# A fused diffusion trunk layer in fp32: rotation tables with the gains multiplied in, differential norms by pairs, row transposes in the middle of a unit, branch weights split in the fourth unit, router logits one unit later

## The reference, cut to what matters

```python
def trunk_layer(l, x, cond, ctx, rope_a, rope_b, p):       # once for 128 prompt rows, once for 512 latent rows
    sh1, sc1, g1, sh2, sc2, g2 = split(silu(cond) @ w_ada + b_ada, 6)
    h = ln_plain(x) * (1 + sc1) + sh1
    aq, ak, av, bq, bk, bv, ga, gb = split(h @ w_in)        # 1024 x 6656
    bq = rms_norm(bq, b_q_g); bk = rms_norm(bk, b_k_g)      # per head of 64
    if rope: aq, ak, bq, bk = apply_rope(each)              # pairs: x1*c - x2*s, x1*s + x2*c
    o_a = diff_attention(aq, kA, vA, lam)                   # 8 heads, two maps: softmax1 - lam * softmax2
    #     then rms_norm(o, subln_g) * (1 - lambda_init), per head of 128
    o_b = gqa_attention(bq, kB, vB)                         # 16 query heads, 4 key heads
    merged = sigmoid(ga) * (o_a @ w_br_a) + sigmoid(gb) * (o_b @ w_br_b)
    x = ln_affine(ALPHA * x + g1 * (merged @ w_o), ln1_g, ln1_b)
    h = ln_plain(x) * (1 + sc2) + sh2
    y = hier_moe(h)     # router logits h @ [w_coarse | w_fine]; best group, its two best experts of four, of 16 in all
    return ln_affine(ALPHA * x + g2 * y, ln2_g, ln2_b), (ak, av, bk, bv)
```

## Time and profile before

| | |
|---|---|
| median of 3 runs | 1377.57 us (1375.84 to 1379.34) |
| the profiled execution's own time | 1376.48 us |
| its span, first to last instruction | 1374.6 us |
| mean granted TensorE clock | 0.952 |
| TensorE matmul busy | 1241.4 us (90%) |
| TensorE weight loads busy | 998.6 us (73%) |
| VectorE busy | 964.2 us (70%) |
| ScalarE busy | 657.8 us (48%) |
| GpSimd busy | 205.9 us (15%) |
| chain that ended last | TensorE 80%, VectorE 10%, DMA 4% |

### The profile page before, as it was taken

One profiled execution on the slowest core, in us unless ns is written; L12 is line 12 of the kernel. 1 busy time (PEld: TensorE's weight loads), 2 busy tenths in 40 slices (PEclk: granted clock), 3 DMA queues, 4 the chain that ended last, 5 costly groups with the idle time before them and its releaser, 6 DMA issues.

```text
span 1374.6 us, 20497 instructions
## 1 busy us (share of the span) xinstructions
PE 1241.4 (90%) x6673; PEld 998.6 (73%) x6673; DVE 964.2 (70%) x1746; ACT 657.8 (48%) x1049; POOL 205.9 (15%) x312
## 2 busy tenths in 40 slices
PE   7999999999999899998997999993699999999940
PEld 4777777777888788887876787773588888888830
DVE  5765521838571688888878535778889999999938
ACT  1522222223322577776763222113478888888812
POOL 0023221020232000011111001000111111122101
PEclk9999999999999999999999999995799999999975
DMA  9877664462646678642005433436899999999925
GB/s 348 283 245 238 207 222 169 153 214 85 201 137 187 180 195 223 187 128 85 27 25 182 131 120 138 169 144 252 299 332 370 372 381 391 388 382 381 336 108 146
DMA packets 150338, 301.05 MB, mean 219 GB/s; under 512 B 20380, under 2 KB 31196, under 8 KB 150264
## 3 DMA queue, kind: packets, MB, share of 16 engines
q1 hardware_dynamic: 122424, 232.72, 49.5%
q0 software_dynamic: 21920, 62.13, 14.5%
q10 hardware_dynamic: 5920, 5.24, 1.3%
HBM read 258.71 MB, written 53.38 MB: 227 GB/s over the span
## 4 chain that ended last, share of the span: by engine, by line
PE 80%; DVE 10%; DMA 4%; issue 2%; ACT 2%; SPq 1%; POOL 0%; DVEq 0%; POOLq 0%; ACTq 0%
PE psum_pair L1705 8%; PE psum_pair L1707 8%; PE psum_pair L1706 8%; PE psum_pair L1807 6%; PE psum_pair L1968 5%; PE psum_pair L1970 5%; PE psum_pair L1969 5%; PE psum_pair L1872 4%; PE psum_pair L1873 3%; PE psum_pair L1874 3%; PE psum_pair L1818 3%; PE psum_pair L1833 3%; PE psum_pair L1983 3%; PE psum_pair L1985 3%; PE psum_pair L1984 3%
## 5 line engine op out<-in xcount | busy, mean ns | idle before, releaser
L1705 PE MATMUL psum_pair<-w_parts,h_hi 128*128 128x512 f32 x520 | 207.8, 400 | 3.0 <-DVE h_lo L1253 3.0
L1707 PE MATMUL psum_pair<-w_parts,h_lo 128*128 128x512 f32 x520 | 204.2, 393 | 0.0
L1706 PE MATMUL psum_pair<-w_parts,h_hi 128*128 128x512 f32 x520 | 203.9, 392 | 0.0
L1110 DVE TENSOR_TENSOR w_parts<-w_raw,w_parts 128x1024 fp32r<-128x1024 f32 x72 | 83.3, 1220 | 91.2 <-ACT w_parts L835 91.1
L975 ACT ACTIVATE p_unnormed<-psum_pair,minus_max 128x640 f32<-128x640 f32 (+1 forms) x160 | 113.4, 712 | 67.2 <-DVE minus_max L1325 65.9
L1807 PE MATMUL psum_pair<-k_bundle,q_bundle 128*128 128x512 f32 (+1 forms) x576 | 123.2, 342 | 13.9 <-ACT p_unnormed L975 9.4
L1325 DVE TENSOR_REDUCE minus_max<-psum_pair 128x1 f32<-128x640 f32 (+1 forms) x160 | 111.8, 715 | 31.4 <-PE psum_pair L1807 28.9
L1705 PEld LDWEIGHTS psum_pair<-w_parts,h_hi 128*128 128x128 f32 x520 | 98.5, 189 | 30.9 <-issue 11.6
L1707 PEld LDWEIGHTS psum_pair<-w_parts,h_lo 128*128 128x128 f32 x520 | 98.4, 189 | 21.1
L1807 PEld LDWEIGHTS psum_pair<-k_bundle,q_bundle 128*128 128x128 f32 x576 | 88.6, 194 | 33.8 <-issue 20.6
L1706 PEld LDWEIGHTS psum_pair<-w_parts,h_hi 128*128 128x128 f32 x520 | 98.6, 190 | 19.7
(11 more groups left out here) (338 smaller groups left out, 2569.5 us busy)
## 6 DMA issues: line engine op xcount, KB each, us to landing
w_raw<-in_w_gate_up SPq DMA_DIRECT2D x76, 512.0 KB, 9.1
w_raw_c<-in_w_gate_up SPq DMA_DIRECT2D x72, 512.0 KB, 10.1
w_raw_b<-in_w_down SPq DMA_DIRECT2D x72, 512.0 KB, 9.2
w_raw<-in_w_in SPq DMA_DIRECT2D x52, 512.0 KB, 8.9
ada_raw<-in_w_ada SPq DMA_DIRECT2D x32, 512.0 KB, 7.4
k_bundle<-k_transposed SPq DMA_DIRECT2D x28, 384.0 KB, 8.5
q_transposed<-turned_staging POOLq DMA_DIRECT2D x40, 256.0 KB, 6.2
ada_raw_early<-in_w_ada SPq DMA_DIRECT2D x16, 512.0 KB, 8.8
```

What stands on the lines that cost most here:

```text
L1110: dve.tensor_tensor(w_parts[b % 2][:, 1, c], w_raw[:, c], w_parts[b % 2][:, 0, c].bitcast(F32), ALU.subtract).then_inc(lo_done, 1)
L1705: pe.matmul(out, a_hi, hi, start=kk == 0, stop=False)
L1706: pe.matmul(out, a_hi, lo, start=False, stop=False)
L1707: return pe.matmul(out, a_lo, hi, start=False, stop=kk == KD - 1)
```

## The change

Seven edits. (1) `gain_tables` multiplies the rotation tables by the gains once, and bq and bk of latent rows are rotated by those tables, without the product with the gain. (2) `norm_o` becomes `norm_sum` (one tile) and `norm_rows` (one or two tiles at once); tiles 1 and 2 and tiles 3 and 4 are normed as pairs, and the order on VectorE and ScalarE at the start of the branches is written out. (3) `turn_o(v + 1)` stands in the middle of unit v (after 6 of 8 steps for v = 0, after 4 otherwise). (4) The branch weights' next block is split at v % 5 == 3 instead of 0. (5) The first unit of each block waits for the weights chunk by chunk. (6) The logits of tile tt - 2 stand between the two halves of tile tt; the last two come at the end. (7) `take_logits` follows suit.

```diff
+        cos_g = sb("rope_cos_gain", [P, 2, TL, HD], F32, s12)
+        sin_g = sb("rope_sin_gain", [P, 2, TL, HD // 2], F32, s12)
+        nsin_g = sb("rope_minus_sin_gain", [P, 2, TL, HD // 2], F32, s12)
...
-        for tt in range(NT + 1):
-            if tt < NT:
-                tail_no["wo", tt, 0], tail_no["wo", tt, 1] = n, n + 1
-                n += 2
+        for tt in range(NT):
+            tail_no["wo", tt, 0] = n
+            n += 1
+            if tt >= 2:
+                tail_no["L", tt - 2] = n
+                n += 1
+            tail_no["wo", tt, 1] = n
+            n += 1
...
@@ ScalarE
-                        act.wait_ge(on_done, z)
+                        act.wait_ge(osum_done, z)
...
-                    square(v + 2)
-                if v % NT == 0:
+                if v == 0:
+                    square(2)
+                if v == 1:
+                    square(3)
+                    square(4)
+                if v % NT == 3:
                     split_hi(branch_block(v) + 1)
...
@@ VectorE
+            def gain_tables():
+                for i, g in enumerate((g_q, g_k)):
+                    halves = g[:].rearrange("p (e two) -> p e two", two=2)
+                    dve.tensor_tensor(cos_g[:, i], cosd[:], over(g[:], 1, [P, TL, HD]), ALU.mult)
+                    dve.tensor_tensor(sin_g[:, i], sind[:], over(halves[:, :, 0], 1, [P, TL, HD // 2]), ALU.mult)
+                    link(dve.tensor_tensor(nsin_g[:, i], nsin[:], over(halves[:, :, 1], 1, [P, TL, HD // 2]), ALU.mult))
...
-                        link(dve.tensor_tensor(qn[:, 0:w].rearrange(s3, d=HD), qn[:, 0:w].rearrange(s3, d=HD),
-                                               over(gain[:], 1, [P, nh, HD]), ALU.mult))
-                        rope(dst, qn[:, 0:w], nh, tt, None)
+                        g = 0 if kind == "bq" else 1
+                        rope(dst, qn[:, 0:w], nh, None, cos_g[:, g, tt], sin_g[:, g, tt], nsin_g[:, g, tt])
...
+                if i == first_v:
+                    gain_tables()
...
+            def norm_sum(z, i):
                 dve.wait_ge(osq_done, z + 1)
+                dve.tensor_reduce(oms[:, i], sqb[:].rearrange("p (h d) -> p h d", d=P), AX.X, ALU.add).then_inc(osum_done, 1)
+                dve.wait_ge(osum_done, z + 1)
+            def norm_rows(z, tiles):
+                link(dve.tensor_scalar(oms[:, 0:tiles], oms[:, 0:tiles], 1.0 / P, EPS, ALU.mult, ALU.add))
+                rsqrt(dve, link, ors[:, 0:tiles], oms[:, 0:tiles], ohf[:, 0:tiles], osh[:, 0:tiles])
+                for i in range(tiles):
+                    o = oin[:, (z + i) % OS].rearrange("p (h d) -> p h d", d=P)
+                    dve.tensor_tensor(o, o, over(ors[:, i], 2, [P, A_HEADS, P]), ALU.mult).then_inc(on_done, 1)
+                dve.wait_ge(on_done, z + tiles)
...
-            norm_o(1)
-            for v in range(4 * NT):
+            norm_sum(1, 0)
+            rest_o(0)
+            norm_sum(2, 1)
+            norm_rows(1, 2)
+            rest_o(1)
+            norm_sum(3, 0)
+            merge(0)
+            norm_sum(4, 1)
+            rest_o(2)
+            norm_rows(3, 2)
+            merge(1)
+            for v in range(3, 4 * NT):
                 if v < 2 * NT:
                     rest_o(v)
-                if v:
-                    merge(v - 1)
-                if v < 2 * NT:
-                    norm_o(v + 2)
-                if v % NT == 0:
+                merge(v - 1)
+                if v % NT == 3:
                     split_lo(branch_block(v) + 1)
...
                 first_sum(tt)
+                if 2 <= tt < NT - 1:
+                    take_logits(tt - 2)
                 if tt:
                     root(tt - 1, 1)
...
-                    take_logits(tt - 1)
+                if tt == NT - 1:
+                    take_logits(tt - 2)
+            take_logits(NT - 2)
             root(NT - 1, 1)
             second_factor(NT - 1)
             take_logits(NT - 1)
...
@@ TensorE
+            def three_passes(out, a_hi, a_lo, b, first, begin, end):
+                for kk in range(begin, end):
+                    if first and kk % 2 == 0:
+                        pe.wait_ge(lo_done, NC_CH * b + kk // 2 + 1)
...
-                if v:
-                    turn_o(v + 1)
                 wait_bank(n)
-                pe.wait_ge(lo_done, NC_CH * (b + 1))
...
-                three_passes(bank(n), ot_hi[br][:, :, cols], ot_lo[br][:, :, cols], b, KD).then_inc(pj_ready, 1)
-                if v == 0:
-                    turn_o(1)
+                middle = KD - 2 if v == 0 else KD // 2
+                three_passes(bank(n), ot_hi[br][:, :, cols], ot_lo[br][:, :, cols], b, tt == 0, 0, middle)
+                turn_o(v + 1)
+                three_passes(bank(n), ot_hi[br][:, :, cols], ot_lo[br][:, :, cols], b, tt == 0, middle, KD).then_inc(pj_ready, 1)
...
+            for tt in range(NT):
+                out_project(tt, 0)
+                if tt >= 2:
+                    logits(tt - 2)
+                out_project(tt, 1)
                 if tt == 0:
+                    turn_columns()
                 if tt == 1:
+                    sum_weights()
                 if tt:
+                    turn_x1(tt - 1)
+            logits(NT - 2)
+            turn_x1(NT - 1)
+            logits(NT - 1)
```

More of the change, by code:

```diff
@@ L1134, in rope @@
                 dve.tensor_tensor(rt[:, 0:w].rearrange("p (m d) -> p m d", m=nh), xs,
[L1135 to L1137 removed]
+                                  over(cos, 1, [P, nh, HD]), ALU.mult)
+                dve.tensor_tensor(uv[:, :, :, 0], xv[:, :, :, 1], over(minus_sin, 1, [P, nh, HD // 2]), ALU.mult)
+                last = dve.tensor_tensor(uv[:, :, :, 1], xv[:, :, :, 0], over(sin, 1, [P, nh, HD // 2]),
                                          ALU.mult)
@@ L1253, in _ @@
                     dve.tensor_tensor(h_lo[:, k], h_mod[:, k], h_hi[:, k].bitcast(F32), ALU.subtract).then_inc(h_done, 1)
+            first_v = [u[0] for u in units].index("v")
             for i in range(N_EARLY, len(units)):
@@ L1353, in _ @@
                 if j == N_A + 40:
-                    norm_o(0)
+                    norm_sum(0, 0)
+                    norm_rows(0, 1)
                     dve.wait_ge(gcol_in, 16)
@@ L1873, in three_passes @@
                     pe.matmul(out, a_hi[:, kk], lo, start=False, stop=False)
-                    last = pe.matmul(out, a_lo[:, kk], hi, start=False, stop=kk == nk - 1)
+                    last = pe.matmul(out, a_lo[:, kk], hi, start=False, stop=kk == KD - 1)
                 return last
@@ L1894, in _, with out_project @@
             turn_merged(NT - 1)
[L1895 to L1904, removed]
+            def out_project(tt, h):
+                n = tail_no["wo", tt, h]
+                b = NB - 2 + h
+                wait_bank(n)
+                pe.wait_ge(tr_free[(TR_M + tt) % 2], (TR_M + tt) // 2 + 1)
+                cols = slice(tt * P, (tt + 1) * P)
+                three_passes(bank(n), ot_hi[0][:, :, cols], ot_lo[0][:, :, cols], b, tt == 0, 0, KD).then_inc(pj_ready, 1)
@@ new lines, in turn_columns, with sum_weights @@
+            def turn_columns():
+                n = tail_no["columns"]
+                wait_bank(n)
+                pe.wait_ge(s4b_in, S4B_IN)
+                pe.transpose(bank(n)[:, 0:4 * KD], mod_c[:], ident[0:4 * KD, 0:4 * KD]).then_inc(pj_ready, 1)
+            def sum_weights():
+                n = tail_no["rows"]
+                wait_bank(n)
+                pe.wait_ge(pj_free[tail_no["columns"] % 4], tail_no["columns"] // 4 + 1)
+                pe.wait_ge(ones_done, 1)
+                for k in range(KD):
+                    last = pe.matmul(bank(n)[:, 0:4 * NR], ones[:], w_rm[:, k].rearrange("p i e -> p (i e)"), start=k == 0, stop=k == KD - 1)
+                last.then_inc(pj_ready, 1)
@@ new lines, in turn_x1, with logits @@
+            def turn_x1(q):
+                pe.wait_ge(x1_done, q + 1)
+                turn_rows(TR_H + q, yb[:, q % 2])
+            def logits(q):
+                n = tail_no["L", q]
+                wait_bank(n)
+                pe.wait_ge(tr_free[(TR_H + q) % 2], (TR_H + q) // 2 + 1)
+                for k in range(KD):
+                    last = pe.matmul(bank(n)[:, 0:NR], h2t[:, k], w_rm[:, k, 0 if q == PROMPT else 1], start=k == 0, stop=k == KD - 1)
+                last.then_inc(pj_ready, 1)
@@ L1905, in _ @@
+            for tt in range(NT):
[3 more added lines that the diff above has]
+                out_project(tt, 1)
                 if tt == 0:
-                    n = tail_no["columns"]
-                    wait_bank(n)
-                    pe.wait_ge(s4b_in, S4B_IN)
-                    pe.transpose(bank(n)[:, 0:4 * KD], mod_c[:], ident[0:4 * KD, 0:4 * KD]).then_inc(pj_ready, 1)
+                    turn_columns()
                 if tt == 1:
-                    n = tail_no["rows"]
@@ L1912, in _ @@
-                    wait_bank(n)
```

(16 more changed lines are left out.)

29 lines of the change are left out of this document (9 added, 20 removed).

## The result

The changed kernel took 1366.3 us in the median of 4 runs (1364.97 to 1368.31), the kernel before 1376.84 (4 runs, 1375.84 to 1379.34): ratio 0.9916, 95% interval 0.9896 to 0.9935. The profiled execution took 1364.97 us, span 1363.0, 11.6 under the span of before; 15.3 were forecast.

What follows compares the result with a forecast made beforehand. TensorE was taken as the bound in most stages, but short of work at the branches' start and around the output projection. Gains 4.2 + 4.2 + 0 + 6.9 = 15.3 us gave a median of 1362.3 us, range 1359 to 1371.

Steps and rivals of the forecast that it cites:

- (a): Favoured case, whole kernel: the gains come as forecast, 1359 to 1366 us; chance 0.65.
- (e): Whole kernel: one part does nothing for an unseen cause, 1366 to 1371 us; chance 0.07.
- (b): Clock falls as often as now: 1.7 us less in projections, 1.7 at 864, 3.3 in tail; 1369 us, chance 0.2.
- Tables: Projections: rotation tables shorten TensorE's wait and avoid a clock fall; gain 4.2 us, bounds 2.3 and 4.4.
- The stall: Projections: TensorE's 2.67 us wait for a turned_staging difference at 273.84 shrinks to 0.13, gaining 2.54 us.
- Branches: Branch stage: earlier unit 0 and fewer waits, less the moved split's price; gain 4.2 us, 5.0 at full clock, lower bound 2.5.
- the term that carries them: Branch stage: a unit of 24 products takes 5.5 us, read from two units between 883.23 and 894.24.
- Output projection: Up to the first row: idle moves to the shift and scale rows' transpose; gain 0, up to 1.7 us lost if the clock falls.
- Tail: Logits one unit later remove waits and clock loss: 7.15 us, net 6.9 after one more small-operation pair; bounds 5.0 and 7.1.
- Routing and experts: After the tail: they begin from the last row, no fixed date seen, so the gain carries one to one.
- (c): Experts: the weight stream sets the end and absorbs the gain, 1374 to 1378 us; chance 0.05.
- (d): Branch units given a turn run at 1.2 GHz, each costing 5.5 us more; units 0 to 3 give 1384 us; chance 0.03.

Runs made afterwards that it cites:

- The single variants: The changed kernel with one of two branch-stage steps undone: turns ahead, 1367.96 us, or single norms, 1368.85 us.
- turns ahead: The changed kernel with the turns of the differential rows put back ahead of the units: 1367.96 us, ratio to before 0.9927.
- both kernels that did it: The changed kernel with the shift and scale rows' transpose behind the second tile's first block, 1364.77 us; the same plus weight splits over two units, 1360.50.
- tables alone: The kernel before with only the rotation tables (edit 1): 1372.86 us, ratio 0.9959.
- branches alone: The kernel before with only the branch stage's part (edits 2 to 5): 1377.14 us, ratio 0.9988.
- single norms: The changed kernel with the differential rows' factors worked out one tile at a time again: 1368.85 us, ratio to before 0.9949.

## Why the prediction was right, and where it was off

The median of 1366.3 us lies in the stated range of 1359 to 1371, on the slow side. By the bands of the rivals it is 0.3 us outside (a), the favoured one, and inside (e), "one part does nothing"; but the runs refute the mechanism of (e), as every part shortens its own stage, and bear out that of (a) with some terms too large and one fall of (b).

**Tables, 4.2 forecast, 3.7 measured** (mean of the projections in the four traces without them 411.5, in the nine with them 407.8). The stall shrank to 0.17 (0.13 forecast) and over the eight microseconds behind it the clock was 1.00, not 0.79. With 2.5 us from the stall, 1.2 are left for the clock, where 1.7 had been forecast.

**Branches, 4.2 forecast, 3.2 measured.** Every wait came in its place: 2.65 ahead of unit 0 (2.48 forecast), 1.29 ahead of unit 1 (1.05), turn of rows 3 late by 0.54 (0.6), unit 4 by 0.35 (0.4), unit 9 by 1.81 (2.1), the load of rows 4 and pairs in time. Off was the term that carries them: from the first turn to unit 1 took 13.26 us and not 12.8, to unit 4 34.2 and not 33.2, to unit 9 64.1 and not 62.8. About 0.5 us was lost ahead of unit 1 already: unit 0 starts 3.74 us after the first turn and not 3.57, and from the turn of rows 1 to unit 1 it takes 3.73 us and not 3.45. The rest is the unit's length. In both kernels the units of the second block stand 5.60 us apart where nothing waits (those of the third, 10 to 14, 5.44), 0.1 more than I read from two half units of the tail, and the forecast counts eight units after and three before (its unit 9 of before stood 0.3 late as well, so 1.0 of the 1.3 is missing). The single variants show what the working had not told: that 4 us hang on pairs and mid-unit turns together.

**Output projection, 0 forecast, with 1.7 as bound.** The wait of 1.8 us (2.0 forecast) is there; the bound became the fact: 1.5 lost in two of three traces of the changed kernel, nothing in one. The sum had taken it at nothing, and against rival (b) I had argued from one stretch of before, where a 1.49 us gap brought no fall. That is the step that failed: one trace without a fall doesn't show that a place is safe. It is a piece of rival (b), one fall and not three.

For the waits in the middle of the branch stage (0.54, 0.35 and 1.81 us) the sum counted no fall, and in all three traces of the changed kernel none came. With the turns ahead, the same 1.81 us at unit 9 brought one. So such a wait is a risk, not a certainty.

**Tail, 6.9 forecast, 7.3 less 0.3.** The rows come 13.67 us apart, as forecast, TensorE has no idle time between them and VectorE still waits 0.7 us a row for TensorE's second half unit, so it keeps pace; the first two tiles' logits after, with no wait ahead of them:

```profile
879.95 1.86 PE L1962 MATMUL psum_pair<-router_weights_modulated,h_turned 128*128 128x20 f32 x16
...
893.62 1.86 PE L1962 MATMUL psum_pair<-router_weights_modulated,h_turned 128*128 128x20 f32 x16
```

The last logits are taken 12.58 earlier against 12.87 for the fourth turn; the 0.29 between is the extra pair of small operations on VectorE (0.27 forecast):

```profile
930.11 0.23 DVE L1477 SCALAR_TENSOR_TENSOR logits<-logit_rows,rows_minus_mean,psum_pair 128x20 f32<-128x20 f32 x1
```

**Routing and experts carry the gain on**, as forecast: the rest takes 403.9 to 405.1 us in the traces without the logits' part or with it alone and 403.3 to 406.2 in the others.

**The sum.** By the stage tables 3.7 + 3.2 + 7.3 less 0.3 behind the tail, less 1.5 in two of three, is 13 us; the timed ratio says 11.6 (8.9 to 14.3). Rival (c) is out, and (d): in the changed kernel no unit with a turn ran slow but unit 0, whose fall was forecast. Open is how often the clock falls at that transpose and on what it depends, and why the keys and the clock in attention differ so much from one execution to the next (266 to 274 us, more than any single part of this change gains); with four traces without the tables and nine with them, no effect of the tables on attention can be told (means 268.5 and 269.2).

## What to carry to other kernels

Compare traces by the lengths of stages between the same instructions, not by their times from the start: here the kernel's own start and its attention moved by 1.7 and 8 us between executions, while the branches and the tail repeated within 0.3 and 0.1. Price a wait that stands in front of a long row of products twice, once for its length and once, as a chance, for a fall of the clock behind it; moving a thin step to where products are ready took that wait away in both kernels that did it, and left a shorter one further on (1.32 and 0.63 us). Two steps that each look right can be worth nothing alone, as the pairs and the mid-unit turns here. Work that is split by chunks can be spread over two units, so that VectorE's share stays under the unit's time in each.

## What the runs showed of the hardware

Whether the granted clock falls behind an idle time is not always settled by the program. At the transpose of the shift and scale rows the changed kernel had the fall behind 1.81 and 1.77 us and not behind 1.67; other kernels had it there behind 1.85 and not behind 1.54, 1.63 and 1.92. So the length of the idle time alone doesn't settle it either.

At other places the fall came in every trace. Unit 0's first eighteen products took 5.8 us, at a granted clock of 0.71, in all eight traces that have a turn behind them (the changed kernel's three among them), where eighteen take 4.2 in units 5 to 8. TensorE had idled 2.65 us before them each time. With the logits where they stood before, four turns of x follow each other in the tail: the second of the three steps between them and the third took 16.6 us (granted clock 0.90 with the tables alone) in all four traces of that order, each with an idle time of 1.19 us in it. The first step has the same idle time; it took 15.0 us in three of the traces and 16.6 in that of the branches alone.

Each fall cost about 1.6 us (unit 4 with single norms took 7.2 us and not 5.55, the first step of the tail 16.6 and not 15.0).
